# Key and value pieces of the odd layer as seven half-block products, with the bias additions in steps

## The reference, cut to what matters

```
q, k, v = jnp.split(h @ w_in, 3, axis=-1)          # w_in is 1024 x 3072
kc, vc = jnp.split(hc @ w_in[:, C_WIDTH:], 2, axis=-1)
...
s_loc = q . kw * C_SCALE + bias                     # 16 columns around each, 4 rows of 64
s_ctx = q . kc * C_SCALE
p = softmax(concatenate([s_loc, s_ctx]))
o = p_loc . vw + p_ctx . vc
y = o @ w_out
```

## Time and profile before

| | |
|---|---|
| median of 3 runs | 2081.95 us |
| the three runs | 2070.73, 2085.36, 2081.95 us |
| profiled execution, first to last instruction | 2082.8 us |
| PE busy in it | 1934.9 us (93%) |
| DVE busy in it | 652.8 us (31%) |
| mean granted clock of TensorE | 0.989 of full speed |

### The profile page before, as it was taken

One profiled execution on the slowest core, in us unless ns is written; L12 is line 12 of the kernel. 1 busy time (PEld: TensorE's weight loads), 2 busy tenths in 40 slices (PEclk: granted clock), 3 DMA queues, 4 the chain that ended last, 5 costly groups with the idle time before them and its releaser, 6 DMA issues.

```text
span 2082.8 us, 33820 instructions
## 1 busy us (share of the span) xinstructions
PE 1934.9 (93%) x14647; PEld 1203.4 (58%) x14647; DVE 652.8 (31%) x1517; ACT 364.7 (18%) x809; POOL 322.1 (15%) x264
## 2 busy tenths in 40 slices
PE   6989999999999989998999988888789999989998
PEld 4565566555555555546555444444376677675884
DVE  1343472222222242115421111111154131047752
ACT  3142410000000021213210000000020220042231
POOL 0143411000000100116110000000020060040120
PEclk9999999999999999999999999999999999999999
DMA  9694499999999988217599999999874414327221
GB/s 350 157 366 165 156 365 400 427 428 426 426 426 426 427 337 237 91 59 296 212 380 426 427 427 426 426 426 426 363 276 160 157 49 161 121 82 203 82 93 61
DMA packets 136109, 590.93 MB, mean 284 GB/s; under 512 B 19410, under 2 KB 35818, under 8 KB 111248
## 3 DMA queue, kind: packets, MB, share of 16 engines
q1 hardware_dynamic: 119536, 564.45, 68.7%
q10 hardware_dynamic: 10304, 17.83, 2.7%
q0 software_dynamic: 6112, 6.39, 0.9%
HBM read 576.95 MB, written 25.33 MB: 289 GB/s over the span
## 4 chain that ended last, share of the span: by engine, by line
PE 67%; DMA 22%; DVE 4%; issue 3%; POOL 2%; ACT 2%; SPq 0%; DVEq 0%; POOLq 0%; ACTq 0%
DMA RG<-in_moe_w 20%; PE banks L1594 13%; PE banks L2666 8%; PE banks L1619 6%; PE banks L1139 4%; PE banks L2261 4%; PE banks L2668 4%; PE banks L1570 4%; PE banks L2263 3%; PE banks L2867 3%; PE banks L3078 2%; PE banks L712 2%; DMA mods_rows<-AR 2%; PE banks L355 2%; POOL AR L957 1%
## 5 line engine op out<-in xcount | busy, mean ns | idle before, releaser
L1594 PE MATMUL banks<-RG,HT 128*64 128x256 f32 x3616 | 426.5, 389 | 35.9 <-DMA RG<-in_moe_w 33.2
L1594 PEld LDWEIGHTS banks<-RG,HT 128*64 128x64 f32 x3616 | 252.0, 134 | 222.1 <-DMA RG<-in_moe_w 56.2
L1873 POOL DMA_INDIRECT y_rows<-AR x64 | 63.9, 998 | 838.3 <-DVE AR L1633 809.9
L1603 DVE TENSOR_TENSOR AR<-AR,banks 128x256 f32<-128x256 f32 x64 | 38.6, 603 | 479.4 <-ACT AR L1599 428.2
L1619 PE MATMUL banks<-RG,AR 128*64 128x512 f32 x752 | 171.7, 598 | 3.1 <-DVE AR L1612 3.1
L2666 PE MATMUL banks<-HT,RG 128*128 128x256 f32 x768 | 168.0, 380 | 0.8 <-ACT HT L550 0.8
L2666 PEld LDWEIGHTS banks<-HT,RG 128*128 128x128 f32 x768 | 145.4, 190 | 22.8 <-issue 2.4
L1599 ACT ACTIVATE AR<-banks 128x256 f32<-128x256 f32 x64 | 24.6, 384 | 742.3 <-PE banks L1594 742.3
L1570 PE MATMUL banks<-AR 128*128 128x256 bf16 (+1 forms) x1152 | 149.3, 277 | 1.6 <-DVE AR L1558 1.5
L1570 PEld LDWEIGHTS banks<-AR 128*128 128x128 bf16 x1152 | 108.2, 98 | 33.3 <-issue 18.3
L1619 PEld LDWEIGHTS banks<-RG,AR 128*64 128x64 f32 x752 | 49.8, 136 | 93.8 <-issue 83.6
(11 more groups left out here) (487 smaller groups left out, 2381.3 us busy)
## 6 DMA issues: line engine op xcount, KB each, us to landing
RG<-in_moe_w SPq DMA_DIRECT2D x160, 2048.0 KB, 23.4
AR<-in_moe_w SPq DMA_DIRECT2D x32, 2048.0 KB, 14.5
RG<-in_ada_w SPq DMA_DIRECT2D x24, 2048.0 KB, 10.7
RG<-in_attn_w_in SPq DMA_DIRECT2D x20, 2048.0 KB, 7.7
RG<-in_odd_w_in SPq DMA_DIRECT2D x6, 2048.0 KB, 19.7
RG<-in_ssm_w_in SPq DMA_DIRECT2D x4, 2048.0 KB, 8.8
AR<-y_rows SPq DMA_DIRECT2D x12, 512.0 KB, 6.0
RG<-in_even_w_out SPq DMA_DIRECT2D x2, 2048.0 KB, 12.3
```

The costliest lines, as they stand in the source:

```text
L1594: m = pe.matmul(p[64 * h:64 * h + 64, 256 * i:256 * i + 256], x[:, k, :], w[:, h, k], start=k == 0, stop=k == 7, skip_group_check=True)
L1873: g.indirect_dma_start(y, off, E.Y[b], None, bounds_check=2047, oob_is_err=False).then_inc(*event)
```

## The change

Keys and values with `hf` 0 (512 tokens x 1024 inputs x 512 outputs each) are no longer eight products of half blocks (256 x 512 x 256) but seven, by Strassen's scheme in the form with fewer additions. A class `Seven` holds the blocks: `b11` to `b22` are the quarters of the weight piece, `x[a][kh]` those of `HT`.

- PE does 7 products in each piece, each of 2 x 4 float32 matmuls of 256 columns (16 records), into banks 4, 5 and 6, with a wait between the products.
- DVE makes four sums of the token blocks once (128 x 1024 each, into places not yet used), and for each piece four sums of weight blocks (`t3`, `t2`, `t1`, `t4`, 128 x 1024 each, three of them in place in the slot), and five sums of 128 x 512 out of PSUM (`u2`, `u3` and three quarters of the result).
- ACT copies two things for each piece: the first product (`one`) and the first quarter of the result.
- The additions of the bias become steps of a generator `dve_bias`. They start only in the second piece: three steps within `dve_seven` of the values, and the other five (`run(fill)`) after its last sum. `odd_done` still waits for the last of them.
- The ring slots of the two pieces are given back after the last product instead of the last part.

The core of the diff:

```diff
...
                 for hf in range(2):
                     for c in range(3):
-                        cols(("odd", c, hf), I["odd_w_in"][0], 512 * (2 * c + hf), 512, ("odd_in", c, hf, 3))
+                        cols(("odd", c, hf), I["odd_w_in"][0], 512 * (2 * c + hf), 512,
+                             ("seven", "odd", c, hf, 6) if c and not hf else ("odd_in", c, hf, 3))
...
+            def __init__(self, key, before, w, turned, banks, x, sums, t2, small, scale, outs):
+                self.key, self.before, self.turned, self.scale, self.outs = key, before, turned, scale, outs
+                self.b11, self.b12 = w[:, 0:4, 0:256], w[:, 0:4, 256:512]
+                self.b21, self.b22 = w[:, 4:8, 0:256], w[:, 4:8, 256:512]
+                self.n = n = x[0][0].shape[2]
+                self.banks = [PS[b][:, 0:2 * n] for b in banks]
+                self.t2, (self.one, self.u2, self.u3) = t2, small
+                a, b, c = self.banks
+                self.products = ((a, x[0][0], self.b11, True), (b, sums[1], t2, True), (a, x[0][1], self.b21, False),
+                                 (b, sums[2], self.b12, False), (c, sums[0], self.b11, True), (b, x[1][1], self.b21, False),
+                                 (c, sums[3], self.b22, False))
...
+        def dve_seven_sums(v, key, x, sums):
+            s1, s2, s3, s4 = sums
+            v.tensor_tensor(s3, x[0][0], x[1][0], SUB)
+            vstep(v, v.tensor_tensor(s1, x[1][0], x[1][1], ADD))
+            vstep(v, v.tensor_tensor(s2, s1, x[0][0], SUB))
+            v.tensor_tensor(s4, x[0][1], s2, SUB).then_inc(*ev("seven_sums", *key))
+        def pe_seven_product(pe, Z, i):
+            q, x, w, first = Z.products[i]
+            n = Z.n
+            for j in range(2 if Z.turned else n // 128):
+                for k in range(4):
+                    start, stop = first and j + k == 0, k == 3
+                    if Z.turned:
+                        m = pe.matmul(q[:, n * j:n * j + n], w[:, k, 128 * j:128 * j + 128], x[:, k, :],
+                                      start=start, stop=stop, skip_group_check=True)
+                    else:
+                        m = pe.matmul(q[:, 256 * j:256 * j + 256], x[:, k, 128 * j:128 * j + 128], w[:, k, :],
+                                      start=start, stop=stop, skip_group_check=True)
+            m.then_inc(*ev("seven", *Z.key, i))
+        def pe_seven(pe, Z, landed_, sums):
+            pe.wait_ge(*landed_)
+            if Z.before is not None:
+                pe.wait_ge(*at("seven_11", *Z.before))
+            pe_seven_product(pe, Z, 0)
+            pe.wait_ge(*at("seven_sums", *sums))
+            pe.wait_ge(*at("seven_t2", *Z.key))
+            if Z.before is not None:
+                pe.wait_ge(*at("seven_21", *Z.before))
+            pe_seven_product(pe, Z, 1)
+            pe.wait_ge(*at("seven_one", *Z.key))
+            pe_seven_product(pe, Z, 2)
+            pe.wait_ge(*at("seven_u2", *Z.key))
+            pe_seven_product(pe, Z, 3)
+            pe.wait_ge(*at("seven_t1", *Z.key))
+            if Z.before is not None:
+                pe.wait_ge(*at("seven_12", *Z.before))
+            pe_seven_product(pe, Z, 4)
+            pe.wait_ge(*at("seven_t4", *Z.key))
+            pe.wait_ge(*at("seven_u3", *Z.key))
+            pe_seven_product(pe, Z, 5)
+            pe.wait_ge(*at("seven_22", *Z.key))
+            pe_seven_product(pe, Z, 6)
+        def act_seven(act, Z):
+            act.wait_ge(*at("seven", *Z.key, 0))
+            if Z.before is not None:
+                act.wait_ge(*at("seven_21", *Z.before))
+            act.activation(Z.one, Z.banks[0], ACT.Copy, scale=Z.scale).then_inc(*ev("seven_one", *Z.key))
+            act.wait_ge(*at("seven", *Z.key, 2))
+            act.activation(Z.out(0, 0), Z.shaped(Z.banks[0]), ACT.Copy, scale=Z.scale).then_inc(*ev("seven_11", *Z.key))
+        def dve_seven_t3(v, Z):
+            v.wait_ge(*landed(Z.key))
+            v.tensor_tensor(Z.b12, Z.b22, Z.b12, SUB).then_inc(*ev("seven_t3", *Z.key))
+        def dve_seven_t2(v, Z):
+            v.wait_ge(*at("seven_t3", *Z.key))
+            v.tensor_tensor(Z.t2, Z.b12, Z.b11, ADD).then_inc(*ev("seven_t2", *Z.key))
+        def dve_seven(v, Z, after, fill):
+            a, b, c = Z.banks
+            def add(out, bank, u, event):
+                v.scalar_tensor_tensor(out=out, in0=bank, scalar=Z.scale, in1=u, op0=MUL, op1=ADD).then_inc(*ev(event, *Z.key))
+            next(fill, None)
+            v.wait_ge(*at("seven_t2", *Z.key))
+            v.wait_ge(*at("seven", *Z.key, 0))
+            v.tensor_tensor(Z.b11, Z.b22, Z.t2, SUB).then_inc(*ev("seven_t1", *Z.key))
+            v.wait_ge(*at("seven_one", *Z.key))
+            v.wait_ge(*at("seven", *Z.key, 1))
+            if Z.before is not None:
+                v.wait_ge(*at("seven_12", *Z.before))
+            add(Z.u2, b, Z.one, "seven_u2")
+            if after is not None:
+                dve_seven_t3(v, after)
+            v.wait_ge(*at("seven", *Z.key, 2))
+            v.tensor_tensor(Z.b21, Z.b21, Z.t2, SUB).then_inc(*ev("seven_t4", *Z.key))
+            v.wait_ge(*at("seven", *Z.key, 3))
+            add(Z.u3, b, Z.one, "seven_u3")
+            if after is not None:
+                v.wait_ge(*at("seven_t4", *Z.key))
+                dve_seven_t2(v, after)
+            v.wait_ge(*at("seven_u3", *Z.key))
+            v.wait_ge(*at("seven", *Z.key, 4))
+            add(Z.out(1, 1), Z.shaped(c), Z.shaped(Z.u3), "seven_22")
+            next(fill, None)
+            v.wait_ge(*at("seven", *Z.key, 5))
+            add(Z.out(1, 0), Z.shaped(b), Z.shaped(Z.one), "seven_21")
+            next(fill, None)
+            v.wait_ge(*at("seven", *Z.key, 6))
+            add(Z.out(0, 1), Z.shaped(c), Z.shaped(Z.u2), "seven_12")
...
+        ODD_X = [[HT[:, 4 * kh:4 * kh + 4, 256 * a:256 * a + 256] for kh in range(2)] for a in range(2)]
+        ODD_SUMS = [KT1[:, 4 + 2 * i:6 + 2 * i, :].rearrange("p a (b c) -> p (a b) c", b=2) for i in range(2)] + [
+            ar(6 * KK + KK * i, 4, 256) for i in range(2)]
+        ODD_SMALL = [VV[:, i, 512:1024] for i in range(3)]
+        ODD_T2 = ar(8 * KK, 4, 256)
+        ODD_SEVENS = [Seven(("odd", c, 0), ("odd", 1, 0) if c == 2 else None, where[("odd", c, 0)][0], c == 1, (4, 5, 6), ODD_X,
+                            ODD_SUMS, ODD_T2, ODD_SMALL, 1.0,
+                            [[KT1[:, 2 * b:2 * b + 2, 256 * a:256 * a + 256] if c == 1 else
+                              VV[:, 2 * a:2 * a + 2, 256 * b:256 * b + 256] for b in range(2)] for a in range(2)])
+                      for c in (1, 2)]
...
-            for c in range(3):
-                for j in range(4):
-                    if c == 0 and j == 2:
-                        pe.wait_ge(*at("joined_rows", 2))
-                    pe_odd_part(pe, c, 0, j)
-                    if c == 0 and j == 0:
-                        pe_last(pe, E0, 3)
-                    if c == 0 and j == 2:
-                        for t in (2, 3):
-                            pe_odd_turn(pe, t)
-                if c == 0:
+            for j in range(4):
+                if j == 2:
+                    pe.wait_ge(*at("joined_rows", 2))
+                pe_odd_part(pe, 0, 0, j)
+                if j == 0:
+                    pe_last(pe, E0, 3)
+                if j == 2:
                     for t in (2, 3):
-                        for b in range(2):
-                            pe.wait_ge(*at(*turned_out("mix1", t, b)))
+                        pe_odd_turn(pe, t)
+            for t in (2, 3):
+                for b in range(2):
+                    pe.wait_ge(*at(*turned_out("mix1", t, b)))
+            for Z in ODD_SEVENS:
+                pe_seven(pe, Z, landed(Z.key), ("odd",))
 
         def act_odd(act):
             act.wait_ge(*at("joined_rows", 3))
@@ -2312,22 +2441,38 @@
             for p in range(2):
                 act.dma_start(NM[64 * p:64 * p + 64], K["k_nam"].rearrange("p a b -> p (a b)")[:, 0:384]).then_inc(
                     *dm("bias_tables", p))
-            for c in range(3):
-                for j in range(4):
-                    act_odd_part(act, c, 0, j)
-                    if c == 0 and j == 2:
-                        for t in (2, 3):
-                            act_odd_turned(act, t)
-
-        def dve_odd(v):
+            for j in range(4):
+                act_odd_part(act, 0, 0, j)
+                if j == 2:
+                    for t in (2, 3):
+                        act_odd_turned(act, t)
+            for Z in ODD_SEVENS:
+                act_seven(act, Z)
+
+        def dve_bias(v):
             v.wait_ge(*at("bias_tables", 1))
             v.wait_ge(*at("bias_loads", 1))
             for h in range(0, 16, 2):
                 b = BT[:, h:h + 2, :]
                 v.tensor_tensor(b, b, bc(NM, 1, 2), ADD).then_inc(*ev("bias_out", h // 2))
+                yield
+
+        def dve_odd(v):
+            a, b = ODD_SEVENS
+            for t in (2, 3):
```

(27 more changed lines are left out.)

## The result

The changed kernel took 2088.6 us (median of 20 runs, 2084.18 to 2098.56) against 2081.95 us (20 runs). The ratio is 1.0038, 95% interval 1.0026 to 1.0051: 5.4 to 10.6 us slower, 7.9 us at the middle. Within 1%, as forecast, and inside the range, but more than the 2.3 us of the sum. The profiled execution of the changed kernel took 2092.19 us with a span of 2090.4: the time is 1.8 us above the span, as in the other runs of which both are known. So the profiled execution before took about 2084.6 us (an estimate from that), 2.6 us above its median, and the changed one 3.6.

What follows compares the result with a forecast made beforehand. PE was taken to bound the stage; -0.3 us at the attention's start and +2.6 us for the slow clock gave +2.3 us, so 2081.95 became 2084.3 us, range 2074 to 2091.

Steps and rivals of the forecast that it cites:

- What bounds the stage, and the price of the products: Keys and values: PE alone bounds; fourteen products at 3.44 us make 48.2 us, 6.7 us less than before.
- the fourth rival: Keys and values: other waits bind or products take 3.58 us; start 2.1 us later, 2086.7 us in all; chance 0.08.
- The stall for `t2`: Ahead of the keys' second product: PE stands still 1.92 us until DVE's six additions are done.
- The tail: Behind the last product: 0.75 us sum, five bias additions of 4.43 us, PE idle 5.3 us; attention starts 0.3 us earlier.
- The clock behind the tail: Start of the attention: PE's 5.3 us idle brings a spell at half clock, costing 2.6 us, bounds 0 and 3.4.
- From there on I carry it whole.: After the attention's first units: the +2.3 us stays unchanged to the kernel's end, later transfers shifting with it.
- a spell at the first product: Rival: the 1.92 us stall in the keys also lowers the clock; +4.0 to +5.7 us, say 2086.9 us; chance 0.17.
- terms for the upper end: Whole kernel, about +8.5 us: late start 2.1, long spell 3.4, spell in the keys 1.7 or more.
- The doubt about the rounding: Later stages: rounding of the seven products might move a token to another expert and change their work; no size given.
- No low spell: Rival at the attention's start: the clock stays high after PE's idle; 2081.7 us; chance 0.2.
- the tail doesn't bind: Rival before the attention: bias additions don't hold it, PE starts 4.7 us earlier; 2077.2 us; chance 0.05.
- Page and row: DVE's 1024-column sums: the skill's page gives 1.13 us, the case's row 1.225; by the page 0.6 us earlier.

Runs made afterwards that it cites:

- code moved by 40: Changed kernel plus 80 already satisfied waits on PE ahead of the second block, so all later PE instructions lie 40 places further; ratio to before 1.0013.
- the steps inside alone: Changed kernel with all eight bias additions as steps within the second piece, none behind its last sum; ratio to before 1.0023.
- PE kept busy: Changed kernel with 20 idle matmuls of 128 columns on PE behind the last product, filling about 4.7 us of its idle; ratio to before 1.0022.
- the early sums: Changed kernel with all bias additions inside the second piece and the keys' first two weight sums made before DVE's last evictions; ratio to before 0.9986.
- The two like kernels with the code moved: Changed kernel, all bias additions inside the second piece, later PE code moved 40 places: ratio 0.9989 without, 0.9966 with the keys' first two weight sums made early.

## Why the prediction was right, and what it missed

- *What bounds the stage, and the price of the products.* Right. 3.46 us a product against 3.44; no stalls but the one foreseen, so the fourth rival is refuted too. (The next piece's sum `t2` was ready 11.8 us before PE needed it, at 811.00 against 822.80 us, and not 8; that changes nothing.)
- *The stall for `t2`.* 2.05 us against 1.92. The six sums took as long as worked out: 1.22 us each, from 791.13 us to 798.40. They began 0.2 us later, measured from the start of the keys, than I had it.
- *The tail.* Right: 0.69 + 4.42 us, PE idle 5.21 against 5.3. The saving on PE was all given back: the stage became 0.2 us longer instead of 0.3 shorter, inside the bounds of -1.3 and +2.1. The difference of 0.5 us is the longer stall (0.13), twelve steps of 3.46 instead of 3.44 us (0.2), and the last product, which takes 3.62 us to its end, where the sum had 3.44 for it (0.2).
- *The clock behind the tail.* Right: a spell of 6.9 us, 3.9 us of it on work. It cost 2.0 us in this trace and 2.6 over five traces against nine, as forecast.
- *"From there on I carry it whole."* This is the step that failed. What the change does to time was carried rightly, but a change also moves the code of everything behind it, and I treated later stages as fixed. That cost 4.6 us in the last stage (4.2 from the mark that both share), twice the forecast effect. With it put right (code moved by 40), the measured effect is 2.7 us against 2.3, with an interval from -0.4 to 5.6. The range held the 2088.6 us only because it left room for a spell at the first product and for scatter: for this loss it had no term, and that part is luck. (Its terms for the upper end, 2.1, 3.4 and 1.7 or 3.4 us, add up to 7.2 or 8.9 us, not to 8.5.) One of the idle stretches that the clock's price was read from, the 4.04 us at 1920 us, was itself a stall that comes with the place of the code. The doubt about the rounding did not come true: from the attention to the last stage both traces take the same time (930.4 and 930.5 us).
- *Rivals.* "No low spell" and "the tail doesn't bind" are refuted by the trace. The spell at the first product happened in one profile of the six with that stall, so its chance of 0.17 was fair, but it is not what made the kernel slower: its 2086.9 us lie nearer to the measured time than the forecast does, for another reason.
- *Page and row.* The 1.13 us worked out from the table of the Trainium skill ("VectorE: DVE Perf Modes", "The TRN2 errata") are too short for a sum of 1024 columns: the changed kernel's rows have 1.22 us. The prediction read half of that section of the Trainium skill: it also says that the row under-predicts, and gives (N + 151) / 0.96 for a float32 addition of two tensors, 1.22 us for 1024 columns (an estimate from that page). The trace agrees with that form. The rule of the Trainium skill that an idle array loses its clock ("TensorE: Matmul & The Clock Gate", Part 1) agrees with the trace behind the tail, where 0.50 follows 5.21 us of idle.

What stays open: why the kernels with the steps inside alone and with PE kept busy are 4.8 and 4.6 us slower than before, where their traces have them about 1 us faster. The first shows in the step from the steps inside to the early sums as well, too: 7.7 us by the middles, at least 3 by the ends of the intervals, where the traces give 2 us of stall. The runs' mean low time, worked out from each run's mean clock, is 49.0 us with the steps inside and 38.8 with the early sums as well, and at half rate these 10.2 us are 5.1 us; the two profiles differ in spells far from the change (one of 0.21 x 16 / 0.5 = 6.7 us between 980 and 996 us in the first alone), and nothing shows why. The two like kernels with the code moved are 4.8 us apart, and their intervals overlap.

## What to carry to other kernels

Work taken off the bounding engine is gained only up to the next thing that the following barrier waits for: list everything in the barrier, and ask of each step that is moved what now lies beside it. Cover for a side task (here the bias additions) belongs in the idle time of its engine early, not behind the last dependent step. And when a small change to one stage costs time in a stage that it doesn't touch, look there for a stall without a releaser before explaining it by the change: move the code by some instructions, and move the transfer next to it, and see whether it goes.

## What was not expected of the hardware

- A stall of 1.4 to 2.1 us without a releaser in the middle of a loop of matmuls depends on where PE's instructions lie: on the kernel before it is absent as it stands and with 100 more, present with 208 more; in the changed kernel it is present, and absent 40 places further.
- It also depends on a transfer in flight: with the same code and the 2 MB issued 5.8 us later, measured against the read-out, it was gone.
- A spell at the lower clock followed it in all five traces, and stall and spell together cost 3.9 us in four of them.
- A second stall of this kind, 3.5 to 4.8 us at 1920 us, is there in the kernel before and in every trace with the later code in another place than the changed kernel's, and gone in the five with it there.
